# Attention: in each pair's turn TensorE multiplies the last pair's values between the next scores and this pair's transposes

## The reference, cut to what matters

```python
scores = jnp.einsum('bnqkgd,bnskd->bnkgqs', qb, kb).astype(jnp.float32) * (HEAD_DIM ** -0.5)
...
scores = scores - slopes[:, :, None, None] * dist
scores = jnp.where(valid[None, :, None, None], scores, NEG_INF)
...
probs = jax.nn.softmax(jnp.concatenate([scores, sink_logit], axis=-1), axis=-1)[..., :-1]
out = jnp.einsum('bnkgqs,bnskd->bnqkgd', probs.astype(v.dtype), vb)
```

## Time and profile before

| what | value |
|---|---|
| median of 3 timed runs | 2648.36 us (2648.12 to 2657.18) |
| the profiled execution, its own time | 2653.53 us |
| its span, first to last instruction | 2651.7 us |
| TensorE busy (products / weight loads) | 2538.1 us / 2084.9 us |
| VectorE, ScalarE, GpSimd busy | 1729.9 / 972.5 / 1025.8 us |
| mean granted TensorE clock | 0.984 of full speed |

### The profile page before, as it was taken

One profiled execution on the slowest core, in us unless ns is written; L12 is line 12 of the kernel. 1 busy time (PEld: TensorE's weight loads), 2 busy tenths in 40 slices (PEclk: granted clock), 3 DMA queues, 4 the chain that ended last, 5 costly groups with the idle time before them and its releaser, 6 DMA issues. The chain is left out here.

```text
span 2651.7 us, 34579 instructions
## 1 busy us (share of the span) xinstructions
PE 2538.1 (96%) x12222; PEld 2084.9 (79%) x12222; DVE 1729.9 (65%) x2277; ACT 972.5 (37%) x1770; POOL 1025.8 (39%) x1187
## 2 busy tenths in 40 slices
PE   7999888999999899999989999999999999999898
PEld 6887777788887588888868888877888887788786
DVE  5211884687896175454687667788767777664886
ACT  5221777512211250123353333343333334532432
POOL 2072123387783000012244454334344434443542
PEclk9999999999999899999999999999999999999999
DMA  6483889644428736465434222213322223455465
GB/s 216 136 292 109 166 163 237 212 143 149 153 95 218 172 143 224 168 167 164 143 90 149 88 88 88 72 56 121 102 88 88 72 82 140 168 191 206 149 208 183
DMA packets 322597, 390.99 MB, mean 147 GB/s; under 512 B 52352, under 2 KB 255104, under 8 KB 314368
## 3 DMA queue, kind: packets, MB, share of 16 engines
q1 hardware_dynamic: 276224, 310.65, 39.2%
q10 hardware_dynamic: 40384, 46.72, 5.3%
q0 software_dynamic: 5824, 31.46, 3.4%
HBM read 255.07 MB, written 133.69 MB: 147 GB/s over the span
## 5 line engine op out<-in xcount | busy, mean ns | idle before, releaser
L529 PE MATMUL tl_banks<-gu_b_hi,gu_a_hi 128*128 128x512 f32 x1848 | 727.5, 394 | 33.2 <-DVE gu_b_lo L1984 19.4
L531 PE MATMUL tl_banks<-gu_b_lo,gu_a_hi 128*128 128x512 f32 x1848 | 724.6, 392 | 0.0
L530 PE MATMUL tl_banks<-gu_b_hi,gu_a_lo 128*128 128x512 f32 x1848 | 724.5, 392 | 0.0
L529 PEld LDWEIGHTS tl_banks<-gu_b_hi,gu_a_hi 128*128 128x128 f32 x1848 | 350.0, 189 | 116.4 <-issue 33.8
L531 PEld LDWEIGHTS tl_banks<-gu_b_lo,gu_a_hi 128*128 128x128 f32 x1848 | 350.3, 190 | 73.4
L530 PEld LDWEIGHTS tl_banks<-gu_b_hi,gu_a_lo 128*128 128x128 f32 x1848 | 350.5, 190 | 72.4
L1978 DVE TENSOR_TENSOR gu_a_lo<-gu_raw,gu_a_hi 128x512 fp32r<-128x512 f32 (+1 forms) x340 | 294.8, 868 | 146.6 <-ACT gu_a_hi L1675 146.5
L1675 ACT ACTIVATE gu_a_hi<-gu_raw 128x512 fp32r<-128x512 f32 (+1 forms) x340 | 208.7, 616 | 347.8 <-PE tl_banks L531 295.6
L1350 POOL TENSOR_TENSOR gu_s_one<-gu_raw 128x512 f32<-128x512 f32 (+1 forms) x68 | 91.7, 1348 | 347.6 <-DVE gu_a_lo L1978 210.2
L1363 POOL TENSOR_TENSOR gu_raw<-gu_s_one,gu_raw 128x512 f32<-128x512 f32 (+1 forms) x68 | 97.8, 1438 | 161.2 <-DVE gu_a_lo L1978 160.8
L148 PE MATMUL pi_banks<-pi_feat_hi,pi_w_hi 128*128 128x512 f32 (+1 forms) x344 | 131.2, 381 | 6.1 <-DVE pi_feat_lo L333 6.1
(11 more groups left out here) (315 smaller groups left out, 4974.6 us busy)
## 6 DMA issues: line engine op xcount, KB each, us to landing
gu_raw<-in_w_ffn_gate SPq DMA_DIRECT2D x44, 512.0 KB, 3.8
gu_raw<-in_w_ffn_up SPq DMA_DIRECT2D x44, 512.0 KB, 3.7
gs_w_raw<-in_w_in SPq DMA_DIRECT2D x40, 512.0 KB, 4.4
gates<-gs_gate_out ACTq DMA_DIRECT2D x64, 256.0 KB, 2.9
br_rows<-gates POOLq DMA_DIRECT2D x16, 1024.0 KB, 7.0
gu_raw<-f SPq DMA_DIRECT2D x32, 512.0 KB, 4.0
dn_y<-down_sums SPq DMA_DIRECT2D x16, 1024.0 KB, 5.0
down_sums<-dn_y SPq DMA_DIRECT2D x15, 1024.0 KB, 6.0
```

What stands on the lines that cost most here:

```text
L529: pe.matmul(out, w_hi, x_hi, start=first, stop=False, skip_group_check=again)
L530: pe.matmul(out, w_lo, x_hi, start=False, stop=False, skip_group_check=again)
L531: return pe.matmul(out, w_hi, x_lo, start=False, stop=last, skip_group_check=again)
```

## The change

One call moves. In each turn TensorE now multiplies the last turn's values before it transposes this turn's probabilities, where before it did both in the other order. No instruction is added or taken away, on any engine; VectorE's, ScalarE's, GpSimd's and SyncE's orders are the same as before.

```diff
             b, r = n // TURNS, n % TURNS
             if n + 1 < PAIRS:
                 score(n + 1)
-            turn_probs(n)
             if n:
                 weigh(n - 1)
+            turn_probs(n)
             if b and r == 1:
                 turn_share(b - 1)
             if n in C_AT:
```

## The result

The changed kernel takes 2663.01 us (median of 7 runs, 2659.41 to 2667.29) where the kernel before takes 2652.66 (median of 7 runs beside it and earlier, 2648.12 to 2658.89): ratio 1.0035, 95% interval 1.0023 to 1.0047, so 6 to 12 us slower. The page hardly differs: the chain that ended last has 40% of the span in products (41% before), the mean granted clock is 0.987 (0.984 before). It doesn't find the place.

What follows compares the result with a forecast made beforehand. TensorE was taken as the fullest engine, with a loop through ScalarE setting the pace after the change. The terms 2.9 + 2.9 + 0 + 4.5 = 10.3 us against 2648.4 gave 2659 us, range 2650 to 2672.

Steps and rivals of the forecast that it cites:

- table turns: Fourteen turns waiting for ScalarE's copy out of `t_psum`: from 3.47 to 3.68 us each, 2.9 us more in all.
- twelve plain turns: Twelve turns from 391.2 us: from 2.64 to 2.88 us each, 2.9 us more in all.
- eight turns: Eight turns from 422.9 us: late loads' waits are given back, about nothing in all, bounds -1 to +1 us.
- other turns: The other 30 turns (narrow, with `turn_c`, or masks delayed by VectorE): 0.15 us each, 4.5 us, bounds 0 to 7.2.
- The loop, 2.88: Values, first transposes, first copy, next exponential, second copy, values again: closes once a turn, 2.88 us, chance 0.68.
- Start of values behind scores: On TensorE, values straight behind scores start between 0.65 and 0.97 us after them; 0.90 used in the sum.
- So there is no gain on that side.: Values come earlier on TensorE, but nothing waits for them closely, so no gain.
- Waits, 12 to 18 us: Values on line 2996 wait for ScalarE's copy, 0.2 to 0.6 us in most wide turns, 12 to 18 in all.
- No change: Rival: TensorE is full, so the order of the same work makes no difference; 2648 to 2651 us, chance 0.12.
- The clock: Rival: a new wait in every turn drops TensorE to its lower clock; 2678 us over twenty turns, chance 0.09.
- Longer loop: Rival: a loop link longer than its row, 0.1 us more in some 45 turns; 2663 us, chance 0.08.
- faster: Rival: values between scores and transposes spare one 0.17 us TensorE gap per turn; 2638 us, chance 0.03.

Runs made afterwards that it cites:

- e1: Changed kernel, but only the second three transposes of a turn stand behind the last turn's values: 2650.84 us, ratio to the kernel before 0.9995.
- the extra instruction: One small ScalarE copy of a constant added per turn in either kernel: changed kernel 2674.71 us (ratio to before 1.0083), kernel before 2658.96 us (1.0024).
- e10: Changed kernel, with ScalarE running the copy out of the tables' tile, then both exponentials, then both copies: 2642.95 us, ratio to before 0.9955.
- e9: Changed kernel, with the copy out of the tables' tile moved to the start of ScalarE's round: 2647.78 us, ratio to before 0.9976.
- e4: Kernel before, with the new order only in the 14 table turns: 2655.59 us, ratio to before 1.0010.
- e5: Kernel before, with the new order in all turns except the 14 table turns: 2657.63 us, ratio to before 1.0021.
- e7: Kernel before, with the copy out of the tables' tile moved to the start of ScalarE's round: 2641.73 us, ratio to before 0.9960.

## Why the prediction came out as it did

The mechanism is shown: the place of the wait (e1), its path through ScalarE (the extra instruction, and e10 against e9), its two forms (e4, e5, e9). The parts of the sum, in us, from the table of groups:

| part | predicted | first trace | second trace of before |
|---|---|---|---|
| table turns | +2.9 | +3.57 | +3.57 |
| twelve plain turns | +2.9 | +2.63 | +2.18 |
| eight turns | 0 | +0.49 | +1.47 |
| other turns | +4.5 | 0.0 | +2.35 |
| sum | +10.3 | +6.7 | +9.6 |

- **The loop, 2.88.** It measured 2.91, each link within 0.02 of its row. The twelve turns took 34.3, forecast 34.6.
- **Table turns.** Too small by 0.7. The links summed to 3.68 (measured 3.71), but the 3.47 set against it was the longest kind of table turn without further work on TensorE; most of these took 3.44 or 3.45.
- **Start of values behind scores.** Taken at 0.90 between 0.65 and 0.97; it is 0.90.
- **Eight turns.** The late loads' waits went, as forecast, and two turns of 3.47 and 4.69 became 2.48 and 3.68; the loop took it back, and more: 24.49 instead of the 23.7 forecast.
- **Other turns.** This is the term that was mis-sized: 0.0 or 2.35 instead of 4.5. Part is the base: the trace that the sum was made against had turns 4 to 9 partly at half clock, 2.5 us longer than in the second trace. Part is a step that failed: "So there is no gain on that side." There is one. Where VectorE's masks are late, the transposes used to stand for an exponential with the values queued behind them; now the values fill that time. In the first trace before, turn 14, and in the view of waits, 258 to 470 us:

```profile
303.53 0.31 PEld L2980 LDWEIGHTS at_p_psum<-first_ident,at_probs 128*128 128x128 f32 x3 [0.66 <-ACT at_probs L3189]
```

```profile
PEld at_p_psum L2980 <- ACT at_probs L3189: 5.9, 10, 0.8
```

In the second trace before it is 6.5 us in 11 times; after, 1.2 in 7, each no longer than the usual gap of 0.17. Turns 14 and 26 are 0.78 us shorter together, and so they are in e5, which has the new order in them but not in the 14 table turns. That the values fill this wait is read from these rows; no run tests it alone. How the rest of the term divides stays open.
- **Waits, 12 to 18 us.** 30.1 by the weight loads, 17.1 by the products. The row of the loads counts the usual gap as well, 0.25 behind scores, 41 x 0.25 = 10 us, which leaves 20. The second three transposes no longer wait, as forecast: all six run on end (414.67, x6).
- **No change.** TensorE's work was the same and the time was not. The Trainium skill, page "Perfetto Trace Analysis", section "Identifying the Most-Contended Engine", says of the most-contended engine: "Optimize this engine first." That the same work on it means the same time was the prediction's own reading of this. e7 took no work from TensorE either and gained 0.4%, by the place of a copy on ScalarE, busy for 14.50 of 20 us in the stretch of the earlier trace rows.
- **The clock.** 1.00 over the loop, and from 300 to 460 us as a whole, though TensorE's weight loads stood 0.85 us in every other turn. The Trainium skill, page "TensorE: Matmul & The Clock Gate", section "A second HAM failure mode: psum-queue depth-cycling", describes a clock that such short idle times unsettle; these traces show none of it there.
- **Longer loop, and faster.** The loop was longer by 0.03, not 0.1. No gap was spared: 9.6 us of them now stand at the transposes and 5.2 at the values.
- **The base.** 2659 was reckoned from a median of three runs, 2648.36; seven have it at 2652.66, so the changed kernel's median lies 4 us above the point. The difference forecast, 10.3, is 10.35 between the medians of seven, nearer than its parts deserve, which is luck: traces of one kernel with equal stages (203.09, 203.02) differ by 3.9 us in their spans.

## What to carry to other kernels

When an instruction moves on a full engine, write down the loop that its wait closes with the other engines' fixed orders, add up the links from rows, and compare with what each engine needs alone; shares of busy time show neither. A wait is best placed behind work that doesn't depend on what the waiting engine holds up, and just enough of it: three transposes were enough, none was not. Before moving work on the fullest engine, look at waits that come again and again for the same releaser, here 14 times for one copy: moving that copy was worth more than either order.

## What was not expected of the hardware

- An instruction's busy time on ScalarE overlaps the next one's: the 128x128 copy is recorded at 0.30 us and costs 0.20, the 128x384 copy at 0.49 and costs 0.39 before an exponential.
- A loop over two engines kept its period to 0.01 us over 19 turns, while TensorE's extras, in every second turn, made the scores swing between 2.47 and 3.35.
- The same program was granted 0.85 of full clock over 22.5 us in one execution, part of it at the lower level, 0.50, and 1.00 in another; the six turns there were 2.5 us apart.
